# A conditioning gate moved from GpSimd in one attention branch to VectorE in another

## The reference, cut to what matters

```python
mod = jnp.einsum('bd,de->be', jax.nn.silu(c), w_ada) + b_ada
shift, scale, gate = jnp.split(mod, 3, axis=-1)
h = rms_norm(x, g_pre) * (1.0 + scale[:, None, :]) + shift[:, None, :]
proj = jnp.einsum('bsd,de->bse', h, w_in)
q_mla, kv_a, z_mla, qkv_dil, z_dil, gl_mla, gl_dil = jnp.split(proj, IN_SPLITS, axis=-1)
a = mla_branch(q_mla, kv_a, positions, g_kv, w_kv_b) * jax.nn.silu(z_mla)
bb = dilated_branch(qkv_dil, positions) * jax.nn.silu(z_dil)
merged = jax.nn.sigmoid(gl_mla) * (a @ w_mla_proj) + jax.nn.sigmoid(gl_dil) * (bb @ w_dil_proj)
x = x + gate[:, None, :] * rms_norm(merged @ w_o, g_post)
```

## Time and profile before

| | |
|---|---|
| median of 3 runs | 2722.99 us (2719.79 to 2727.32) |
| span of the profiled execution, first to last instruction | 2713.1 us |
| TensorE busy, mean granted clock | 2604.3 us (96%), 0.978 |
| VectorE busy | 1885.7 us (70%) |
| ScalarE busy | 1100.6 us (41%) |
| GpSimd busy | 1180.7 us (44%) |

### The profile page before, as it was taken

The page is one execution under the profiler, slowest core; times in us unless marked ns, Lnnn a source line. Parts: engine busy times, 40 slices in busy tenths (PEclk is TensorE's granted clock), DMA queues, the critical chain, the costliest instruction groups (busy, mean ns, idle before and its releaser), DMA issues.

```text
span 2713.1 us, 46656 instructions
## 1 busy us (share of the span) xinstructions
PE 2604.3 (96%) x20272; PEld 2354.8 (87%) x20272; DVE 1885.7 (70%) x2270; ACT 1100.6 (41%) x1312; POOL 1180.7 (44%) x656
## 2 busy tenths in 40 slices
PE   6899989998999999999999999999999999999997
PEld 3678867788999999999998899899888888889986
DVE  2249863378988888888897876676546884886554
ACT  2243312244433443434446453443444443444453
POOL 0048731025899999999981575780000000000001
PEclk9889999899999999999999999999999999999998
DMA  9958567876877877777765786885766656666664
GB/s 342 344 154 229 163 228 246 283 198 180 240 240 241 247 237 236 238 239 247 239 212 133 204 223 192 213 223 158 186 192 181 171 171 178 179 165 168 188 184 118
DMA packets 745003, 570.49 MB, mean 210 GB/s; under 512 B 44608, under 2 KB 629440, under 8 KB 744672
## 3 DMA queue, kind: packets, MB, share of 16 engines
q1 hardware_dynamic: 744800, 567.52, 70.9%
HBM read 565.38 MB, written 2.10 MB: 209 GB/s over the span
## 4 chain that ended last, share of the span: by engine, by line
PE 81%; DVE 11%; DMA 2%; POOL 2%; ACT 2%; issue 1%; SPq 0%; DVEq 0%; POOLq 0%
PE bank L848 20%; PE bank L851 10%; PE bank L815 6%; PE bank L816 6%; PE bank L817 6%; PE bank L831 5%; PE bank L835 5%; PE bank L832 5%; DVE w_low L1894 3%; PE bank L1101 2%; PE bank L804 2%; PE bank L886 2%; PE bank L884 2%; PE bank L885 2%; POOL prod L655 1%
## 5 line engine op out<-in xcount | busy, mean ns | idle before, releaser
L1894 DVE TENSOR_TENSOR w_low<-ring,w_high 128x2048 fp32r<-128x2048 f32 (+1 forms) x389 | 951.7, 2448 | 327.4 <-ACT w_high L1437 320.2
L1437 ACT ACTIVATE w_high<-ring 128x2048 fp32r<-128x2048 f32 (+1 forms) x389 | 738.0, 1900 | 334.7 <-DMA ring<-w_up 120.3
L848 PE MATMUL bank<-acts,w_high 128*128 128x512 f32 x2784 | 672.9, 394 | 4.9 <-DVE zs L2010 3.3
L848 PEld LDWEIGHTS bank<-acts,w_high 128*128 128x128 f32 x2784 | 514.3, 189 | 109.3 <-issue 7.8
L655 POOL TENSOR_SCALAR prod<-adf,cact 128x512 f32<-128x512 f32 x165 | 386.5, 2342 | 22.1 <-DMA adf<-w_ada 6.1
L851 PEld LDWEIGHTS bank<-acts,w_low 128*128 128x128 f32 x2784 | 356.9, 191 | 14.6 <-DVE w_low L1894 1.1
L831 PE MATMUL bank<-acts,w_high 128*128 128x256 f32 x1504 | 365.8, 284 | 0.0
L832 PE MATMUL bank<-acts,w_high 128*128 128x256 f32 x1504 | 364.9, 283 | 0.0
L851 PE MATMUL bank<-acts,w_low 128*128 128x256 f32 x2784 | 361.2, 283 | 0.7 <-DVE w_low L1894 0.7
L669 POOL TENSOR_TENSOR sumf<-sqf 128x256 f32<-128x256 f32 x1 | 0.7, 740 | 786.2 <-ACT sqf L1875 786.2
L656 POOL TENSOR_TENSOR acc<-prod,acc 128x512 f32<-128x512 f32 x165 | 288.9, 1751 | 13.8
(11 more groups left out here) (464 smaller groups left out, 4023.9 us busy)
## 6 DMA issues: line engine op xcount, KB each, us to landing
ring<-w_in SPq DMA_DIRECT2D x176, 1024.0 KB, 5.8
ring<-w_up SPq DMA_DIRECT2D x88, 1024.0 KB, 5.9
ada<-w_ada SPq DMA_DIRECT2D x76, 1024.0 KB, 6.6
adf<-w_ada SPq DMA_DIRECT2D x44, 1024.0 KB, 8.1
ring<-w_down SPq DMA_DIRECT2D x44, 1024.0 KB, 6.5
ring<-w_out SPq DMA_DIRECT2D x16, 1024.0 KB, 6.0
adg<-w_ada SPq DMA_DIRECT2D x64, 256.0 KB, 5.2
ring<-w_mla SPq DMA_DIRECT2D x16, 1024.0 KB, 5.5
```

The costliest lines, as they stand in the source:

```text
L848: pe.matmul(o, wh[:, j], both, start=j == 0, stop=False, skip_group_check=True)
L1437: act.activation(WH[s][:, 0:WIDE[n]], ring[s][:, 0:WIDE[n]], ACT.Copy).then_inc(high_done, 1)
L1894: v.tensor_tensor(WL[s][:, 0:WIDE[n]], ring[s][:, 0:WIDE[n]], f32(WH[s][:, 0:WIDE[n]]), ALU.subtract)\
```

## The change

The four turns go from GpSimd in the attention branch to VectorE in the dilated branch. At each list position p from 3 to 66 VectorE does one row, as one multiply-add of 128 x 512 into a single sum `acc_g` (the first row of a turn only multiplies), waits for it, and after every 16th row releases PE. SP loads the row at p = k + 4 ahead of the unit's own load, into one of four buffers. PE sums a turn after the units at p = 18, 34, 50 and 66 (`ROWS_OVER`), ahead of scores or transposes that stand at the same position; VectorE takes the sums one position later. The loop on GpSimd, `gate_rows` on SP and the old places of `ada` and `ada_take` go.

```diff
+ROWS_OVER = {18 + DT * t: t for t in range(4)}
...
-        AG = [at(f"adg{k}", W0 + 100 + 2 * k, [P, 512]) for k in range(2)]
-        prod_g = at("prod_g", W0 + 104, [P, 512])
+        AG = [at(f"adg{k}", W0 + place, [P, 512]) for k, place in enumerate((64, 66, 98, 106))]
+        acc_g = at("acc_g", W0 + 80, [P, 512])
...
+            def gate_row(k):          # SP
+                t, j = divmod(k, DT)
+                if k >= 4:
+                    sp.wait_ge(g_free, k - 3)
+                c = 2 * D + 512 * t
+                sp.dma_start(AG[k % 4][:, :], w_ada2[P * j:P * j + P, c:c + 512]).then_inc(g_landed[k % 4], 16)
...
+            for p, key in enumerate(DILATED):
+                if 4 <= p < 4 + DT * N_LATE:
+                    sp.wait_ge(unit_done, UNIT[DILATED[p - 4]] + 1)
+                    gate_row(p - 4)
...
-            for turn in range(N_LATE):          # GpSimd: the whole loop goes
...
-                    if 4 * half + i in (3, 4, 6):          # PE, attention
-                        ada(acc_g[(3, 4, 6).index(4 * half + i) % 2])
...
+                if p in ROWS_OVER:          # PE, dilated, after the unit's matmuls
+                    ada(acc_g)
                 if p in SCORES_AT:
...
+            def gate_row(k):          # VectorE
+                v.wait_ge(g_landed[k % 4], 16 * (k // 4 + 1))
+                j = k % DT
+                w, col = AG[k % 4][:, :], cact[:, DT + j:DT + j + 1]
+                if j == 0:
+                    v.tensor_scalar(acc_g[:, :], w, col, None, ALU.mult).then_inc(g_free, 1)
+                else:
+                    v.scalar_tensor_tensor(acc_g[:, :], w, col, acc_g[:, :], ALU.mult, ALU.add).then_inc(g_free, 1)
+                v.wait_ge(g_free, k + 1)
+                if j == DT - 1:
+                    v.memset(small[:, 56:57], 0.0).then_inc(ada_sums, 1)
+
             for p, key in enumerate(DILATED):
                 ahead(*key)
+                if p - 1 in ROWS_OVER:
+                    ada_take(8 * DT + 4 * ROWS_OVER[p - 1])
+                if 3 <= p < 3 + DT * N_LATE:
+                    gate_row(p - 3)
                 if p - 1 in SCORES_AT:
```

More of the change, by code:

```diff
@@ L245, in program @@
         prod_e = at("prod_e", 12, [P, 512])
-        AG = [at(f"adg{k}", W0 + 100 + 2 * k, [P, 512]) for k in range(2)]
-        prod_g = at("prod_g", W0 + 104, [P, 512])
-        acc_g = [at("acc_g0", W0 + 106, [P, 2, T])[:, :, :], at("acc_g1", W0 + 99, [P, 10, T])[:, 0:10:9, :]]
+        AG = [at(f"adg{k}", W0 + place, [P, 512]) for k, place in enumerate((64, 66, 98, 106))]
+        acc_g = at("acc_g", W0 + 80, [P, 512])
         CB = [at(f"c_wide{k}", W0 + place, [P, DT, 32]) for k, place in enumerate((107.75, 107))]
@@ L321, in program @@
         ada_sums = sem("ada_sums")
-        g_landed = sems("g_landed", 2)
+        g_landed = sems("g_landed", 4)
         g_free = sem("g_free")
@@ L566, in _ @@
             load(("kv", 4), w_in2[:, 3584:3648], cols=64)
[L568 to L576, removed]
+            def gate_row(k):
[4 more added lines that the diff above has]
+                sp.dma_start(AG[k % 4][:, :], w_ada2[P * j:P * j + P, c:c + 512]).then_inc(g_landed[k % 4], 16)
             for key in ATTENTION + [("gl", k) for k in range(1, 16)]:
@@ L584, in _ @@
                     load(key, w_mla[half * 1024:half * 1024 + 1024, 256 * k:256 * k + 256], kt=8, cols=256)
-                    if not half:
-                        gate_rows(1)
                     continue
@@ L604, in _ @@
                     load(key, cols_of(w_in2, i * 256 + 3648 + half * 1024 + P * h))
-                if half or i:
-                    gate_rows({"kvb": 2, "q0": 1, "q1": 1, "z0": 2, "z1": 2}.get(w, 0))
-            for key in DILATED:
+            for p, key in enumerate(DILATED):
+                if 4 <= p < 4 + DT * N_LATE:
+                    sp.wait_ge(unit_done, UNIT[DILATED[p - 4]] + 1)
+                    gate_row(p - 4)
                 if key[0] == "dv":
@@ L742, in _ @@
             B.up("sq_done", 8)
-            for turn in range(N_LATE):
[L745 to L757, removed]
             summed(sumf, sqf, 14)
@@ L1371, in _ @@
                     proj8(("proj", half, k), k % 4, 4 * half + 4)
-                    if half and k == 2:
-                        ada(acc_g[1])
             for k in range(1, 16):
@@ L2466, in _ @@
                     added(qn[:, 1, :], 3)
-                    if 4 * half + i in (3, 4, 6):
-                        ada_take(8 * DT + 4 * (3, 4, 6).index(4 * half + i))
                     if half == i == 0:
@@ L2523, in _ @@
                     B.up(f"bank_free{k % 4}")
-                    if half and k == 2:
-                        ada_take(8 * DT + 12)
             for s in range(4):
```

## The result

The changed kernel takes 2735.41 us (median of 4 runs, 2728.33 to 2736.32) against 2722.83 for the kernel before beside it: ratio 1.0045, 95% interval 1.0028 to 1.0062, that is 7.6 to 16.9 us more. Two later comparisons gave 1.0063 (1.0044 to 1.0082) and 1.0050 (1.0033 to 1.0067). So it is slower by some 12 to 17 us; 9 were predicted. One of six executions in the third comparison ran 5% longer at a lower granted clock (0.839) and is left out of all numbers here. The profiled execution took 2736.32 us, with a span of 2734.5.

The account below looks back on a forecast made before the run. TensorE (PE) was taken as the bound, busy 96% of the span: -5.2 + 12.8 + 1.5 = +9.1 us on a span of 2713.1 gives 2722.2, with 9.9 us to the runs' median 2732 us; range 2722 to 2741.

Parts of the forecast that it names:

- The gain, 5.2 us: Attention branch without GpSimd's work: 3.3 us of bank waits, 0.75 of a stretched product and 1.1 of clock saved.
- The 1.1 us for a clock that would half hold: End of the attention branch's first half: wait 4.0 instead of 4.8 us, half of the 2.2 us clock cost credited.
- The row, 0.79 us: One 128x512 multiply-add on VectorE in the dilated branch, scaled from the 128x256 one; bounds 0.725 and 0.97 us.
- The stalls, 12.8 us: TensorE's added waits for VectorE in the dilated branch, summed over eight list positions; 11.1 to 17.7 us by row time.
- p = 18: First sum over partitions, dilated branch: TensorE waits 0.4 us for the 16th row.
- p = 34: Second sum, in head 3: TensorE waits 7.2 us, the row 5.2 behind head 2's weights, these 2.0 late.
- p = 27: Dilated branch, a full head behind: TensorE waits 2.0 us for VectorE's softmax.
- p = 50: Third sum, among value units: TensorE waits 0.8 us for the row, including 0.6 for the later load.
- The clock, 1.5 us: Clock falling behind the 7.2 us stall in head 3: between nothing and 2.2 us, 1.5 taken.
- The rows didn't fit: Rival, chance 0.13: a row takes at most 0.5 us, so seven fit in a head; +1.0 us, 2724 us.
- The gain came: Rival, chance 0.11, that it doesn't: attention branch's bank waits and product late for another reason than GpSimd; +14.3, 2737 us.
- The loads were no bound: Rival, chance 0.06, that they become it: dilated branch's loads at 200 GB/s stretch a head to 45.9 us; +18, 2741 us.

Follow-up runs that it names:

- no_rows: The changed kernel without the 64 rows and their loads, sums taken of a zero accumulator: 2715.71 us against 2723.76 for the kernel before.
- pool_dilated: The changed kernel with the rows on GpSimd in the dilated branch, two accumulators and sums three units later: 2725.88 us, ratio 1.0011 to the kernel before.
- late_sums: The changed kernel with two accumulators and the four sums three units later, rows unmoved: 2722.59 us, ratio 1.0003 to the kernel before.
- no_row_loads: The changed kernel without 60 of 64 row loads, the first four rows read again and again: 2734.69 us, ratio 1.0035 to the kernel before.
- last_rows: The changed kernel with only the last row of each sixteen loaded and run: 2726.61 us, ratio 1.0015 to the kernel before.
- the idle matmuls: The changed kernel with 14 unused matmuls where TensorE stands at position 34: 2732.22 us, against 2735.09 for the changed kernel beside it.

## Why the prediction was right, and where it was off

**The gain, 5.2 us.** Right as far as shown: the bank waits went, the product is at 425 ns, the wait of 4.8 became 4.0, and no_rows measured 3.3 to 10.3 us. GpSimd's work and the row loads left the attention branch together, so no run there tells them apart; that GpSimd stretches such operations is shown in pool_dilated. The 1.1 us for a clock that would half hold is not borne out: behind the wait of 4.0 the clock stayed down 5.9, 6.0 and 3.4 us after the restart in the three profiles (4.3 before), and behind the wait of 3.38 us at the end of the second half (the earlier trace rows have it without a fall) it now fell in all three, as it did in no_rows.

**The row, 0.79 us.** Measured: 2083.01 to the next start at 2083.79 (2088.17 to 2088.95 the second time), 0.78 with its wait; 0.747 alone. Scaling the nearest row with its operand was right.

**The stalls, 12.8 us.** Measured, with p = 18: 12.1, 13.3 and 11.7. The sum held, but not every term, so that it came so close is partly luck. p = 34 was 6.67 for 7.2: 4.64 for the place and 2.03 for the lag. The 5.2 of the prediction counts from the weights; from TensorE's own time its rows give 2194.13 - 2189.35 = 4.8. p = 27 was 0.45 for 2.0 and p = 20 nothing for 0.4: TensorE stands at p = 18 and then runs the sum itself, some 2 us in which VectorE catches up, and the prediction added stalls that relieve one another. A head's lag was also over-sized: in late_sums, where no stand at a sum relieves it, p = 27 waits 0.56 and p = 34 1.41. p = 18 was 1.22 for 0.4 and p = 50 2.14 for 0.8; without the row loads they are 0.67 and 1.28, so the loads explain 0.55 and 0.86. The rest at p = 50 is no matter of the rows' loads: the split there waits for a late high half with and without them (3.86 us before, 4.45 in no_row_loads, 4.35 in last_rows), and why it is later against TensorE than before stays open. Of the bounds, 17.7 comes out as 12.8 + 26 x 0.18 = 17.5 by the prediction's own count of rows.

**The clock, 1.5 us.** The term that was mis-sized. Behind p = 34 it cost 3.3 us in the first profile (6.65 us at half), 3.5 in the second and 3.0 in the third, above even the 2.2 that the prediction took as its bound; behind p = 18 another 1.7 in two of three, which the prediction did not have; behind p = 41 and p = 50 more in the second profile. Dilated time against no_rows is 17.0, 23.5 and 14.9 us; less the waits in it (10.8, 12.3, 10.7) that leaves 6.2, 11.2 and 4.2. Half of the time at 0.50 behind the restarts is 5.0, 10.3 and 3.0 of it; about 1 us in each has no name. By the runs, the rows cost 19 to 24 us for the predicted 14.3, and in each profile the clock makes most of what was missing. The gain was 6.8 us for 5.2, so the forecast of the whole lies nearer the result than that of the loss.

**The rivals.** The rows didn't fit (0.747 us, not 0.5). The gain came. The loads were no bound: without 60 of 64 of them the stand at p = 34 was unchanged.

**What stays open.** In all three profiles of the changed kernel, and with the idle matmuls, the clock is also down for some 3.4 us from about 1511 us on, behind a wait of 2.1 us that is 1.8 to 2.0 in the others, where it isn't. That costs 1.7 us, far ahead of any row, and no run here says why.

## What to carry to other kernels

When work moves to an engine that still has idle time, ask where in its order the last piece ends and who stands for it: here one sum ahead of a softmax's turn cost 5 to 10 us, 47 us of added work almost nothing once it lay mostly where that engine waits for loads. A stand of the bounding engine can be worth more than its length, by the clock behind it (here 3.0 to 3.5 us on top of 6.7), and stalls on one path relieve each other, so walk them in order instead of adding them. Before work is moved between two engines, compare the same operation's duration with and without the other engine beside it.

## What the runs showed of the hardware

Rows on GpSimd cost VectorE some 22 us where rows on VectorE itself cost it 30, in operations that read SBUF alone (the split 2290 to 2439 ns), not in those that read a bank. And the same stand of 6.7 us brought the clock down in all four profiles that have it, the three of the changed kernel and no_row_loads, while waits of 1 to 3.4 us did so in some profiles and not in others: at p = 18 it fell behind 1.22 and 0.97 us and stayed at 1.00 behind 1.02.
